# One step of a hybrid attention and expert-retrieval layer: running the two dense expert stages beside each other from tile 80 on

## The reference, cut to what matters

```python
s_top, i_top = lax.top_k(s, PEER_TOPK)          # per half key
best_s, best_j = lax.top_k(cand_s, PEER_TOPK)   # of 16 x 16 sums
expert = jnp.take_along_axis(cand_i, best_j, axis=-1)
gate = jax.nn.softmax(best_s, axis=-1)
pre = jnp.einsum('thkd,td->thk', u[expert], xb)
act = jax.nn.gelu(pre, approximate=False) * gate
return jnp.einsum('thk,thkd->td', act, v[expert])
```

## Time and profile before

| | |
|---|---|
| median of 3 runs | 1874.14 us (1873.4 to 1875.48) |
| the profiled execution | 1875.91 us, of which the span from the first to the last instruction is 1874.1 us |
| first dense stage, tiles 0 to 127 | 597.8 to 1285.9 us |
| second dense stage, places 0 to 127 | 1285.9 to 1860.4 us |
| what follows (last norm, stores) | 1860.4 to 1874.1 us |
| TensorE, VectorE, ScalarE, GpSimd busy | 95%, 77%, 42%, 34% |
| moved by DMA | 478.22 MB |

### The profile page before, as it was taken

The page is one execution under the profiler, slowest core; times in us unless marked ns, Lnnn a source line. Parts: engine busy times, 40 slices in busy tenths (PEclk is TensorE's granted clock), DMA queues, the critical chain, the costliest instruction groups (busy, mean ns, idle before and its releaser), DMA issues.

```text
span 1874.1 us, 26361 instructions
## 1 busy us (share of the span) xinstructions
PE 1777.3 (95%) x9675; PEld 1516.0 (81%) x9675; DVE 1434.5 (77%) x2750; ACT 778.4 (42%) x1555; POOL 644.6 (34%) x409
## 2 busy tenths in 40 slices
PE   6999999989999899999999999978999999999997
PEld 6999776559998899999899999976676666766764
DVE  4433676665678788989999999867888788888787
ACT  3112566553444333333768788522222222222222
POOL 1100000000000133434223366555557566665672
PEclk8999799789999999999999999999999999999998
DMA  6233100002222589989788899999999999999996
GB/s 217 68 131 121 45 1 1 1 1 85 68 77 95 185 305 334 316 307 327 262 276 297 279 387 387 386 400 333 386 389 382 401 387 389 401 402 384 400 379 216
DMA packets 153599, 478.22 MB, mean 255 GB/s; under 512 B 14896, under 2 KB 53808, under 8 KB 149888
## 3 DMA queue, kind: packets, MB, share of 16 engines
q1 hardware_dynamic: 96112, 264.62, 38.7%
q0 software_dynamic: 56928, 208.28, 30.4%
q10 hardware_dynamic: 432, 3.64, 0.5%
HBM read 419.47 MB, written 56.75 MB: 254 GB/s over the span
## 4 chain that ended last, share of the span: by engine, by line
PE 69%; DVE 16%; DMA 8%; ACT 3%; issue 3%; POOL 0%; SPq 0%; ACTq 0%; DVEq 0%
PE ps L1003 17%; PE ps L981 16%; PE ps L633 10%; PE ps L1012 7%; PE ps L918 5%; DMA g_in<-gates_scattered 4%; PE ps L723 3%; DVE hot L1718 3%; DVE w_lo L1339 3%; DVE ring L1737 2%; PE ps L969 2%; PE ps L714 2%; PE ps L766 2%; DMA ring<-u_rows,idx_b 1%; DMA raw<-w_tiles 1%
## 5 line engine op out<-in xcount | busy, mean ns | idle before, releaser
L981 PE MATMUL ps<-md_hi,w_hi 128*128 128x384 f32 x1024 | 358.6, 350 | 36.9 <-DVE w_lo L1339 36.7
L981 PE MATMUL ps<-md_hi,w_lo 128*128 128x384 f32 x1024 | 345.8, 338 | 0.0
L981 PE MATMUL ps<-md_lo,w_hi 128*128 128x384 f32 x1024 | 345.7, 338 | 0.0
L613 POOL DMA_INDIRECT ring<-u_rows,idx_a x128 | 197.2, 1541 | 404.2 <-DVE dots L1737 294.8
L1339 DVE TENSOR_TENSOR w_lo<-raw,w_hi 128x1024 fp32r<-128x1024 f32 x176 | 215.3, 1223 | 79.2 <-ACT w_hi L1265 59.4
L613 POOL DMA_INDIRECT ring<-v_rows,idx_a x128 | 225.1, 1759 | 136.7 <-DVE acc L1747 105.4
L1737 DVE CUSTOM_DVE_ANT_0 ring<-ring,x_n 128x1024 f32<-128x1024 f32 x192 | 230.7, 1223 | 12.7 <-DMA ring<-u_rows,idx_b 10.7
L1747 DVE SCALAR_TENSOR_TENSOR acc<-ring,actg,acc 128x1024 f32<-128x1024 f32 x188 | 234.8, 1282 | 0.0
L981 PEld LDWEIGHTS ps<-md_hi,w_hi 128*128 128x128 f32 x1024 | 194.5, 190 | 46.3 <-DVE w_lo L1339 45.3
L1003 PE MATMUL ps<-w_hi,p_hi 128*128 128x512 f32 x576 | 193.0, 416 | 9.4 <-DVE w_lo L1805 9.1
L981 PEld LDWEIGHTS ps<-md_lo,w_hi 128*128 128x128 f32 x1024 | 194.5, 190 | 0.0
(11 more groups left out here) (265 smaller groups left out, 3261.2 us busy)
## 6 DMA issues: line engine op xcount, KB each, us to landing
raw<-w_tiles SPq DMA_DIRECT2D x176, 512.0 KB, 5.2
v_buf<-v_rows SPq DMA_DIRECT2D x128, 512.0 KB, 11.4
gates_scattered<-g_st SPq DMA_DIRECT2D x24, 1024.0 KB, 6.7
g_in<-gates_scattered SPq DMA_DIRECT2D x32, 768.0 KB, 15.8
activated<-act_st SPq DMA_DIRECT2D x112, 192.0 KB, 4.2
act_in<-activated SPq DMA_DIRECT2D x28, 768.0 KB, 12.9
kv_t<-qkv ACTq DMA_DIRECT2D x3, 1184.0 KB, 4.7
xh<-x_t SPq DMA_DIRECT2D x8, 296.0 KB, 6.0
```

The source lines that it names most:

```text
L613: pool.indirect_dma_start(ring[slot][:], None, u_rows if table == "u" else v_rows, bass.IndirectOffsetOnAxis(ap=idx, axis=0)).then_inc(gat ...
L981: mm = nc.tensor.matmul(ps[:, slot, 0:ND], w[:, slot, kc, :], x[:, kc, :], start=(kc == 0 and j == 0), stop=(kc == KC - 1 and j == 2))
```

## The change

The second dense stage no longer waits for the end of the first. From tile 81 on, TensorE runs place i - 81 (`down`) behind tile i, so that 47 places lie between the last 47 tiles; the other 81 follow. For this

- the scatter starts at tile 25 in place of 64, so that all gates exist by tile 74; D0, D1 and D2 are routed ahead of B; the routing steps and dots get new lines (`STEP_LINE`, and `OP_LINE` for all 384 gathered operations: 82 dots by tile 80, 262 operations by the end of the tiles);
- one-hots are scaled a tile later (in the tile whose matmuls use them), the scatter's matmuls come after the sixth and eighth eighth of the tile, and evacuation a tile later;
- 80 activated tiles go through HBM in place of 112; the 48 of tiles 80 to 127 stay on the chip;
- gates are loaded in 16 groups of 8 tiles, 384 KB a piece, in place of 8 groups of 16 tiles with 768 KB a piece: runs of 512 bytes in HBM in place of 1024. Two pieces are asked for in each of two neighbouring places, from place 53 on as soon as the buffer's last user is done; groups 0 and 1 are asked at tiles 75 and 76, all eight pieces behind each other;
- the fused places have four slots for `v` and one pair of buffers for its split (`v_parts`), later places six slots and two pairs; the loads for the places behind the border are asked ahead of it;
- the first 16 sums of A come ahead of B's sums.

The diff, cut to its core:

```diff
-PLAN = [("top", RT_A), ("sel", RT_B), ("top", RT_B), ("top", RT_D0), ("top", RT_D1), ("sel", RT_D2), ("top", RT_D2)]
+PLAN = [("top", RT_A), ("top", RT_D0), ("top", RT_D1), ("sel", RT_D2), ("top", RT_D2), ("sel", RT_B), ("top", RT_B)]
+RANK = [[b for kind, b in PLAN if kind == "top"].index(s) for s in range(5)]
 N_STEPS = 5 * TOP_STEPS + SEL_STEPS[RT_B] + SEL_STEPS[RT_D2]
-STEP_LINE = [(0, 0), (7, 13), (64, 54), (90, N_STEPS)]
-G_AT = 64
+STEP_LINE = [(0, 0), (7, 13), (21, 26), (37, 39), (53, 57), (72, N_STEPS)]
-G_AT = 64
+G_AT = 25
...
-GL_TILES = 16
+GL_TILES = 8
-DOT_LINE = [(10, 0), (64, 67), (90, 97), (112, 140), (N_EXP, 178)]
+FUSED = 80
+N_FUSED = N_EXP - FUSED
+V_TILES = [*range(FUSED, N_EXP), *range(FUSED)]
+OP_LINE = [(10, 0), (28, 28), (76, 72), (FUSED, 82), (N_EXP, 262), (N_EXP + FUSED, 384)]
...
 OPS = ([("u", 0, k) for k in range(PAIRS)] + [("u", 1, k) for k in range(PAIRS // 2)]
-       + [("v", 1, k) for k in range(PAIRS // 2)] + [("v", 0, k) for k in range(PAIRS)])
+       + [("v", 0, k) for k in range(16)] + [("v", 1, k) for k in range(PAIRS // 2)] + [("v", 0, k) for k in range(16, PAIRS)])
...
-KEPT = GL_TILES
-STORED = N_EXP - KEPT
-V_TILES = [*range(N_EXP - KEPT // 2, N_EXP), *range(STORED, N_EXP - KEPT // 2), *range(STORED)]
+
+V_SLOT, V_LAND, V_PREV = [], [], []
+for place in range(N_EXP):
+    slot = place % 4 if place < N_FUSED else (place - N_FUSED) % V_SLOTS
+    V_LAND.append(16 * (V_SLOT.count(slot) + 1))
+    V_PREV.append(max((p for p in range(place) if V_SLOT[p] == slot), default=None))
+    V_SLOT.append(slot)
...
-                n, tiles = GL_TILES * GB_TOK, (grp - 1) % (N_EXP // GL_TILES)
+                n, tiles = GL_TILES * GB_TOK, (grp + FUSED // GL_TILES) % (N_EXP // GL_TILES)
...
+            def load_v(j):
+                slot, t = V_SLOT[j], V_TILES[j]
+                if V_PREV[j] is not None:
+                    sp.wait_ge(v_done, V_PREV[j] + 1)
+                elif slot < 4:
                     sp.wait_ge(hot_used, N_GRP)
-                elif i < V_SLOTS:
+                else:
                     sp.wait_ge(u_done, N_EXP)
...
+            def beside_place(j):
+                last = min(j + 3, N_FUSED + 3) if j < N_FUSED - 1 else min(j + V_SLOTS, N_EXP - 1)
+                while len(v_asked) <= last:
+                    load_v(len(v_asked))
+                    v_asked.append(j)
+                if j == N_FUSED - 4:
+                    for s in act_stored:
+                        sp.wait_ge(s, 16 * (FUSED // 4))
+                    sp.wait_ge(v_done, N_FUSED - 4)
+                    load_acts(0)
+                if j >= N_FUSED and j % 4 == 0:
+                    sp.wait_ge(v_done, j)
+                    g = (j - N_FUSED) // 4 + 2
+                    for g in range(1 if j == N_FUSED else g, min(g + 1, FUSED // 4)):
+                        load_acts(g)
+
+                first = 0 if j < N_FUSED + GL_TILES // 2 else 5
+                k = (j + GL_TILES + first // 5 * 3) // GL_TILES
+                if j % GL_TILES in (first, first + 1) and 2 <= k < N_EXP // GL_TILES:
+                    sp.wait_ge(p_made, (k - 1) * GL_TILES)
+                    for piece in range(2):
+                        load_gates(k, 2 * (j % GL_TILES - first) + piece)
...
+                if i == G_END + 1:
+                    for j in range(4):
+                        load_v(j)
+                        v_asked.append(j)
                 if i == G_END + 2:
                     for s in g_stored:
                         sp.wait_ge(s, 16 * (N_GB // 2))
-                if G_END + 2 <= i < G_END + 6:
-                    load_gates(0, i - G_END - 2)
-                if G_END + 7 <= i < G_END + 11:
-                    load_v(i - G_END - 7)
-
...
-                if i % 16 in (0, 3, 6, 9) and i < N_EXP - 16:
-                    if i >= 16:
-                        sp.wait_ge(p_made, i // 16 * 16)
-                    load_gates(i // 16 + 1, i % 16 // 3)
+                    for piece in range(4):
+                        load_gates(0, piece)
+                if i == G_END + 3:
+                    for piece in range(4):
+                        load_gates(1, piece)
+                if i > FUSED:
+                    beside_place(i - FUSED - 1)
+
+            for i in range(N_FUSED - 1, N_EXP):
+                beside_place(i)
...
+            def down(i):
+
+                if i in SPLIT:
+                    q = SPLIT.index(i)
+                    hi, lo = v_parts(i)
+                    pe.wait_ge(p_ready, q + 1)
+                    pe.wait_ge(v_ready, q + 1)
+                    for t in range(3):
+                        for n, (p, v) in enumerate(((p_hi, hi), (p_hi, lo), (p_lo, hi))):
+                            for h in range(2):
+                                mm = nc.tensor.matmul(ps[:, 2 + 2 * t + h, :], p[:, q % 3, t * P:(t + 1) * P],
+                                                      v[:, 512 * h:512 * h + 512],
+                                                      start=(i == 0 and n == 0), stop=False)
+                    mm.then_inc(v_done, 1)
+                    return
+                pe.wait_ge(p_made, i + 1)
+                pe.wait_ge(v_in[V_SLOT[i]], V_LAND[i])
+                for t in range(3):
+                    for h in range(2):
+                        mm = nc.tensor.matmul(ps[:, 2 + 2 * t + h, :], acts(i)[:, t * P:(t + 1) * P],
+                                              v_buf[V_SLOT[i]][:, 512 * h:512 * h + 512],
+                                              start=False, stop=(i == N_EXP - 1))
+                mm.then_inc(v_done, 1)
...
-                    if kc == 1 and now:
+                    if kc == 5 and now:
                         scatter(now[0])
-                    if kc == 4 and now:
+                    if kc == 7 and now:
                         scatter(now[1])
...
+                if i == FUSED:
+                    pe.wait_ge(g_evac, N_GRP)
+                if i > FUSED:
+                    down(i - FUSED - 1)
+
+            for i in range(N_FUSED - 1, N_EXP):
+                down(i)
...
+            def v_high(i):
+
+                if i in SPLIT:
+                    q = SPLIT.index(i)
+                    act.wait_ge(v_in[V_SLOT[i]], V_LAND[i])
+                    before = q - (1 if i < N_FUSED else 2)
+                    if before >= 0 and (SPLIT[before] >= N_FUSED or i < N_FUSED):
+                        act.wait_ge(v_done, SPLIT[before] + 1)
+                    elif i >= N_FUSED:
+                        act.wait_ge(u_done, N_EXP)
+                    nc.scalar.copy(v_parts(i)[0][:], v_buf[V_SLOT[i]][:]).then_inc(v_hi_ready, 1)
...
-                for g in groups_of(i, 0):
+                for g in groups_of(i, 1):
                     scale_hots(g)
-                for g in groups_of(i, 1):
+                for g in groups_of(i, 2):
                     take_gates(g)
+                if i > FUSED:
+                    p_high(i - FUSED - 1)
+                    v_high(i - FUSED - 1)
                 act.wait_ge(u_done, i + 1)
...
+                if i >= FUSED + 8:
+                    act.wait_ge(v_done, i - FUSED - 7)
+                dst = act_st[:, i % 4] if i < FUSED else acts(i - FUSED)
                 nc.scalar.activation(dst, ps[:, i % 2, 0:ND], ACT.Gelu).then_inc(act_done, 1)
...
+            def v_low(i):
+
+                if i in SPLIT:
+                    q = SPLIT.index(i)
+                    dve.wait_ge(v_hi_ready, q + 1)
+                    before = q - (1 if i < N_FUSED else 2)
+                    if before >= 0:
+                        dve.wait_ge(v_done, SPLIT[before] + 1)
+                    hi, lo = v_parts(i)
+                    TT(lo[:], v_buf[V_SLOT[i]][:], hi[:].bitcast(F32), SUB).then_inc(v_ready, 1)
...
             for i in range(N_EXP):
+                if i > FUSED:
+                    product(i - FUSED - 1)
                 for g in groups_of(i, 0):
...
-                for s in range(along(DOT_LINE, i), along(DOT_LINE, i + 1)):
+                if i > FUSED:
+                    p_low(i - FUSED - 1)
+                    v_low(i - FUSED - 1)
+                for s in ops_of(i):
                     gathered(s)
```

243 lines of the change are left out of this document (99 added, 144 removed).

## The result

The changed kernel took 1905.70 us (median of 5 runs, 1900.06 to 1909.59), the kernel before 1875.48 (5 runs, 1873.40 to 1876.39): a ratio of 1.015, 95% interval 1.0121 to 1.0178. It is slower, as forecast, and inside the range, but by 30 us where the forecast said 13. The profiled execution took 1908.44 us, its span 1906.6.

The account below looks back on a forecast made before the run. TensorE, busy 95% of the span, was taken as the bound, with 53 us idle or slowed. New losses of 42 + 12 + 5 + 2 + 4 = 65 us, plus 1 for small steps, made 13 us slower: 1887 us, range 1860 to 1914.

Parts of the forecast that it names:

- VectorE in tiles 11 to 73: Tiles 11 to 73: 369 us of VectorE work against 350.7 of TensorE make VectorE the bound; 29 us lost.
- The first rival: Early tiles not VectorE-bound: tiles 11 to 73 lose no more than 23 us, total 1867 us; decided at 26; chance 0.20.
- the sign to look for: VectorE busy over 95% from tile 25 to 57, with tiles there every 6.6 to 6.9 us.
- The exponentials: At tiles 20, 36, 52 and 71 ScalarE waits for VectorE's last step, delaying scalings: 13 us, bounds 4 and 24.
- The burst: Tiles 75 to 81: 14.2 MB of queued transfers make tile 81 wait for `raw`, 12 us, range 3 to 14.
- The border: At place 48 activations of group 1 wait for place 47, and product 52 needs them three places later: 2 us.
- The gates' smaller pieces: Gate reads in 512-byte runs: old group waits go, shorter runs cost nothing; 4 us kept for the range.
- The pairs: 47 tile-and-place pairs at 8.6 us each: VectorE's waits for gathers cost 0.1 us a pair, 5 us in all.
- the ring sets the pair's pace: Gathers landing in 9.5 us make pairs about 9.2 us: 28 us lost instead of 5, total 1910 us; chance 0.18.
- the rival of transfers that bound all behind tile 74: 302 MB behind tile 74 at 376 GB/s take 803 us, 15 more than TensorE: 1878 us; chance 0.03.
- The change leaves TensorE's matmuls as they are: Whole kernel: TensorE's matmuls stay the same, so the 53 us of idle or slowed TensorE is all it can win.
- The change moves losses and no more: Rival: what the burst costs less is paid at the routing; 1874 us within 4; chance 0.13.

Follow-up runs that it names:

- e6: Changed kernel with work left out: the first 72 dots multiply and add 256 of their 1024 columns; 1876.35 us.
- e11: Changed kernel with the first 72 dots cut to 256 of 1024 columns and the exponentials behind the scalings in ScalarE's list; 1867.21 us.
- e16: Changed kernel with exponentials behind the scalings and, for all blocks but the first, a tile later, with divisions, transposes and copies; 1888.35 us.
- e2: Changed kernel with gate pieces read from other places (wrong gates, same bytes) in runs of 3072 bytes instead of 512; 1890.34 us.
- e8: Changed kernel with some 13 gathers moved out of tiles 74 to 81, places 1 to 47 taking 183 operations instead of 176; 1908.68 us.
- e9: Changed kernel with gates stored by group, so pieces are read in runs of 3072 bytes and stores write runs of 512; 1892.53 us.
- e12: Changed kernel with exponentials behind scalings, activations ahead of `v`, gates stored by group, and dots shifted from burst and pairs to the last places; 1885.38 us.
- e14: Changed kernel with exponentials behind scalings and a tile later, activations ahead of `v`, gates stored by group, first gate pieces one at a time; 1869.93 us.

## Why the forecast was right in kind and short in size

**VectorE in tiles 11 to 73: right.** 369 us of work were forecast and 371.76 measured, and taking 53 us of it away (e6, e11) gave 25 to 27 us back for the 29 forecast. The first rival (a loss of 26 us at most) falls with it. Only the sign to look for was wrong: not all tiles run at 6.6 to 6.9 us; most run at 6.0, and single ones pay.

**The exponentials: right in mechanism, a little small.** 13 us forecast, 16 by e16, inside the bounds of 4 and 24.

**The burst: mis-sized, 12 us forecast, 19.3 measured.** The wait for `raw` itself was right (12.6 us on TensorE for 12), and e2 and e8 speak for bytes rather than the queue: without the first hold `raw` was issued sooner and still late, and with 13 gathers fewer half of the loss went. Left out were place 0, which waits 2.9 us more, and the clock: 0.77 from 1090 to 1112.

That is a fault of every new term that was a wait (the exponentials, the burst, the border): the old losses were read from lengths of stretches, in which the slow matmuls behind each stop are counted, these terms were sums of waits alone. At tile 36 the difference is 1.9 us on 6.7.

**The border: the step that failed.** "2 us" counted the wait for place 47 and the product at 52. In SyncE's list the load of activations stands behind loads of `v`, the last of which waits for the end of place 48 (its issues run from 1517.71 to 1527.31), and the load then takes 12.40 us. Measured are 8.6 us, and 3.0 to 7.2 with the order turned; so the order is a part of it, and the landing time and the fallen clock are the rest.

**The gates' smaller pieces: the other step that failed.** I took nothing for them and left 4 us to the last places for other causes. They cost 12 us there (7.8 against -4.6, in e2 and e9 alike; at the new pace 12.8 against 0.5). The old waits for gates did go, as forecast; the price shows at the loads of `v`, for which ScalarE waits 38.5 us, and 3.8 in e9. The same 124 MB went in 54,558 packets and in 33,907, and SyncE's packets took 183 us of the engines' time and 167. By the Trainium skill, page "DMA: Bandwidth & Descriptors", section "Specifications", 512 bytes still run at line rate. Here the trace does not agree, with 16 us more of the engines' time for the same bytes. The stretch with runs of 1024 bytes, by which I chose, did not show it either.

**The pairs: too high, 5 us forecast and -2.1 measured.** VectorE did wait for the ring, 40.5 us in all, and had room for it; by the new pace the pairs lose 1.0. But e8 comes near the rival "the ring sets the pair's pace": with 183 operations for 176 the pairs lose 11.3 us, by the ring or by the transfers. And the rival of transfers that bound all behind tile 74 has a true core: e8 and e12 could empty the burst only at the price of the pairs or the last places. (Its sum was off: the loads and gathers that it lists make 297 MB, not 302, and at 376 GB/s 791 us, 3 us more than TensorE and not 15.)

**A term that was not there.** "The change leaves TensorE's matmuls as they are" holds for their number, not for their time: 32 fours of places at 17.43 us for 17.70 are some 8.6 us less, which nobody forecast and no run explains. That the sum did not miss by more is luck to this extent: the waits grew by that much more than the losses show.

"The change moves losses and no more" falls: the sum grew by 29.6 us. Of the 17.6 us that the forecast lacks in the losses, 10.4 are the border and the last places, 7.3 the burst, 7.0 the early tiles, less 7.1 at the pairs. What stays open is the rest of tiles 11 to 73 with both causes lightened (11.9 us in e11) and how much of e14's gain each part holds, since the medians of one kernel (the one before) differ by up to 3 us between the chips. Open too are how the 12 us of the short reads divide, and what the second hold of SyncE costs in the burst.

## What to carry to other kernels

A term that is a wait on TensorE costs more than the wait: read old losses and new terms in the same unit, lengths of stretches. Where an issue is moved, read the whole list of its queue ahead of it, with every wait in it, not only the wait that guards it. When two engines and the transfers are full at once, moved work shows its price at the place it is moved to; and an outlier tile holds both its own stop and the lateness that it lets others make up, so that only taking the cause away tells its price.

## What the runs showed of the hardware

- Behind a stop of 6.69 us TensorE ran at a granted clock of 0.50 (1.2 GHz), and eight scatter matmuls took 2.08 us; the next eight, with the clock at 0.96 over their window, took 1.06.
- Reads in runs of 512 bytes instead of 3072, 12.6 of the 124 MB of the last places (32 pieces of 384 KB), cost 12 us of 340 with the DMA engines at a share of 0.99, and 16 us more of the engines' time; writes in runs of 512 bytes cost nothing where the share was 0.84.
- An issue of a gate piece in 768 runs held SyncE's queue for 0.38 to 8.79 us, one in 128 runs for 0.33 to 2.18 (e2). An issue of 512 KB of `v` among the former held it for up to 9.80 us, among the latter (e9) for 0.34 at most.
- In the burst a load of `raw` that was issued 13 us sooner in its queue landed 18.91 us after its issue instead of 9.2.
- Four places of the same matmuls take 17.70 us in one kernel and 17.43 in the other, both at a granted clock of 1.00.
- The early stretch of the same instructions started between 660.5 and 670.8 us after the span's start.
